# A network on one core: start-up loads in landing order, one weight block at a time in the first feed-forward, latent scores in pairs, copies before reciprocals

## The chip, the core and the metric

One NeuronCore of a Trainium2 chip runs the whole program in one launch. TensorE multiplies, VectorE, ScalarE and GpSimd do the elementwise work, and the queue of SyncE (SP) starts nearly all loads. The metric is device time in microseconds (us): median of 3 runs of the kernel before 2950.37 us (2949.48 to 2950.72).

## The reference

Two large blocks (`first_block`, layers l = 0, 1) and then four smaller mixer layers, on 256 tokens of width 1024, in float32. The parts that the change touches:

```python
# first_block, per layer
mod = silu(c) @ ada_w[l] + ada_b[l]          # (1024) x (1024, 9216): 9 vectors, shift/scale/gain of three norms
h = rms_norm(x) * norm_ffn1[l] * (1 + sc1) + sh1
x = x + 0.5 * (1 + g1) * ((silu(h @ ffn1_w1[l]) * (h @ ffn1_w3[l])) @ ffn1_w2[l])
...
# mla: 8 heads, latent attention; q, k have 128 plain and 64 rotary dimensions per head
s = causal(q @ k.T) * 192 ** -0.5;  p = softmax(s);  o = p @ v
# second part: i = 0..3, mixers NSA, MOBA, short convolution, NSA; in NSA 16 heads x 2 branches
# (selected and window) = 32 score jobs, in MOBA 16 heads = 16 jobs of head dimension 64
```

## The kernel before

**Weights.** Every weight matrix comes in units of 1 MB (a slab of 1024 x 256), in one list `units` in the order of use. `sync_program` walks through the list: unit u goes into `raw[u % 4]` as soon as unit u - 4 is used up (`freed`). A "split" unit is then converted: ScalarE rounds it into the high half of `wsp` (`ready_act`), VectorE subtracts to get the low half (`ready_dve`; in the trace "TENSOR_TENSOR wsp<-raw,wsp"), and TensorE multiplies with high and low halves. There are three `wsp` buffers. `reach(u)` says how far along the list the conversions may go when unit u has been multiplied; it is computed once and gives both engines their order.

**The adaLN units.** `ada_w` makes 72 units (j = 0..71). The first eight are the first units of the list. Even ones (`fresh`) go straight from `raw` to TensorE in `ada_pe` (64 matmul records of one column each, "P<-sm,raw"); odd ones are summed on VectorE in eight steps into an accumulator (`ada_step`, "ACC<-raw,sm"), and TensorE only turns the result (four matmuls, "P<-C,ACC"). `mod_dve` adds the bias; after j = 7 the shift and scale of the first norm are there. So each of the first loads is freed by TensorE (even j, semaphore `AMM`) or VectorE (odd j, `ARED`). Before the change TensorE takes them as 0, 1, 2, ... 7, and VectorE starts on j = 1 only after the reciprocal of the first norm.

**First feed-forward.** `norm_dve` makes the normalised input in chunks (h_scaled, then high part on ScalarE, low part on VectorE; the marks `HLO`). `ffn_pe` multiplies block i of `w1` and `w3` (`f1`, `f3`); for i = 0 it takes both blocks at once through `lins`: chunk by chunk, both weight units per chunk. PSUM banks are handed out in a fixed order by `take`, `take2` and `give`; a bank comes with the marks that must have been reached before it is written.

**Latent attention (MLA).** 8 jobs, one per head. `attend_pe` is software-pipelined by steps i: scores of job i (two products, of 128 contraction rows and of 64 rows, each for 256 and for 128 columns), transposes of the softmax of job i - 3, values of job i - 4. VectorE takes scale, mask and row minimum (L88, "CUSTOM_DVE_ANT_0") and the reciprocal of the sum, ScalarE the exponential and the copy of the transposed tile, GpSimd the scaling (L79). The rotary part of head h lies on partitions 0 to 63 for even h and 64 to 127 for odd h.

**NSA and MOBA attention.** `attend2_pe/act/dve` take two jobs per step; here VectorE also copies the transposed tiles (L94, "arena<-P 128x384"). Its order per job: row minimum, reciprocal of the job before, copy of job i - 4, and at the last job of a chunk the low part of the output of job i - 6 ("GX<-P,GX").

Every engine's program is written out in this order; there is no run-time scheduler.

Of the kernel before, what the change touches and what calls it, by code (L numbers as in the profile page):

```python
# [109 lines left out]
def build(nc, A, cst, out):  # L110
    ctx = ExitStack()
    with ctx:
# [188 lines left out]
        def reach(u):  # L301

            s, a, r = sum(x <= u for x in splits), sum(x <= u for x in U["ada"]), u
            while r + 1 < len(units):
                x = r + 1
                if x in nsplit and nsplit[x] - NS >= s or units[x][3] == "ada" and nada[x] - 2 >= a:
# [70 lines left out]

        def ada_step(e, j, q):
# [3 lines left out]
            if q == 0:  # L382
                e.wait_ge(*RAW[u % NR].at(u))
                e.wait_ge(*COND_.at("cond"))
                if j >= 2:
                    e.wait_ge(*AMM.at(j - 2))
                e.tensor_scalar(ACC[j % 2][:, :], w[:, 0, :], COND[:, 0:1], None, ALU.mult).then_inc(*ARED.up((j, 0)))
            else:
                e.wait_ge(*ARED.at((j, q - 1)))
                e.scalar_tensor_tensor(ACC[j % 2][:, :], w[:, q, :], COND[:, q:q + 1], ACC[j % 2][:, :], ALU.mult,  # L390
# [214 lines left out]
        def start_dve(e):  # L605
# [8 lines left out]
            for q in (1, 2):  # L614
                square_dve(e, 0, q)
            root_dve(e, 0)
            ready_dve(e, -1)
# [67 lines left out]
        def ada_pe(e, j):  # L685
# [11 lines left out]
            else:  # L697
                e.wait_ge(*ARED.at(j))
                e.wait_ge(*c_in.at("c"))
                for q in range(2):  # L700
                    for x in range(2):
                        ins = e.matmul(P[b][half(x), q:q + 1], ACC[j % 2][:, 128 * q + 64 * x:128 * q + 64 * x + 64], one,
# [90 lines left out]
        def spread_pe(e, n):  # L793
# [5 lines left out]
            give(("nspr", n), NR_.at(n) if late(n) else HT_.at((n, 3)))  # L799
# [93 lines left out]
        def ffn_pe(e, f, n):  # L893
            for i in range(NB):
# [880 lines left out]
        def attend_pe(e, a, jobs, base, steps=None):  # L1775

            SM_, PP, PT = att_tiles(base)
            n = len(jobs)
            for i in steps or range(n + 4):
                if i < n:  # L1780
                    j = jobs[i]
                    b = take(e, ("as", a, i))
                    for m in j["after"]:
                        e.wait_ge(*m)
                    last = len(j["q"]) - 1
# [4 lines left out]
                    ins.then_inc(*ASCO.up((a, i)))  # L1790
                    give(("as", a, i), AMX.at((a, i, 1)))
# [150 lines left out]
        def attend2_dve(e, a, jobs, base, scale, steps):  # L1942
            SM_, PP, PT = att_tiles(base)
            n = len(jobs)
            for i in (x for s in steps for x in (2 * s, 2 * s + 1)):
                if i < n:
# [13 lines left out]
                if 4 <= i < n + 4:  # L1960
                    t = i - 4
                    e.wait_ge(*ATR.at((a, t)))
                    if t >= 4:
                        e.wait_ge(*AVL.at((a, t - 4)))
                    e.tensor_copy(PT[t % 4], P[bank["at", a, t]][:, 0:384]).then_inc(*ACPV.up((a, t)))
                if i >= 6 and jobs[i - 6]["last"]:
                    ch = jobs[i - 6]["chunk"]
                    e.wait_ge(*AHI.at((a, ch)))
                    e.tensor_tensor(gL[:, ch, :], P[bank["av", a, ch]][:, 0:256], gH[:, ch, :].bitcast(F32),
                                    ALU.subtract).then_inc(*ALO.up((a, ch)))  # L1970
# [50 lines left out]
        def mla_pe(e, l):  # L2021
# [94 lines left out]
        def mla_act(e, l):  # L2116
# [57 lines left out]
            attend_act(e, l, jobs, 9728, range(0, 2))  # L2174
            ready_act(e, U["gb", l][2])
            gate_b_act(e, l, 3)
            for i in range(2, 12):
# [551 lines left out]
        def tensor_program(e):  # L2729
# [3 lines left out]
            for j in range(8):  # L2733
# [3 lines left out]
                if j == 1:  # L2737
                    spread_pe(e, 0)
# [187 lines left out]
```

## Time and profile before

| | |
|---|---|
| median of 3 runs | 2950.37 us |
| profiled execution, its own time | 2951.04 us |
| its span | 2949.2 us |
| mean granted TensorE clock | 0.981 of full |
| TensorE / weight load / VectorE / ScalarE / GpSimd busy | 96% / 85% / 71% / 49% / 5% |
| chain that ended last | TensorE 83%, VectorE 9%, ScalarE 5%, DMA 1% |

The start of the span is where the first loads and the first norm stand: the first large matmul begins at 52.73 us. The two MLA attentions begin near 567.6 and 1360.4 us, the attentions of the four mixer layers near 1716, 2043 and 2670 us (the short convolution has none). A timeline row gives the start, the length, engine, line of the code (a helper's line, so tiles tell more), operation, out<-in, how many instructions are merged (xN), and in brackets the idle time before it with what ended it. A matmul in float32 leaves two records (two passes).

### The profile page before, as it was taken

To read this page: it belongs to the slowest core of one execution; us is meant where nothing else is said; L and a number is where in the kernel's file an instruction comes from. 1 tells how busy PE (TensorE), PEld (TensorE's weight loads), DVE (VectorE), ACT (ScalarE), POOL (GpSimd) and SP (SyncE) were. 2 spreads that over 40 slices of the span, in tenths; PEclk is the share of its full clock that TensorE was granted. 3 is DMA by queue.
4 is the path that set the end of the run, shared out by engine and by line. 5 is a ranking of instruction groups with operands and counts; after the bars stand their busy time and mean duration, and the time that the engine had idled before them with its cause. 6 is when DMAs were issued, how large, how long until landed. Compare 5 with 4: busy or idle time off the path is not lost.

```text
span 2949.2 us, 53560 instructions
## 1 busy us (share of the span) xinstructions
PE 2826.3 (96%) x22724; PEld 2513.7 (85%) x22724; DVE 2083.9 (71%) x3259; ACT 1457.5 (49%) x1957; POOL 150.7 (5%) x257
## 2 busy tenths in 40 slices
PE   5999999999999999999999999999899999999998
PEld 5888899888888888998888878889788988887887
DVE  5986857668778868666776587754676677657774
ACT  2545644555445466445454365543554345436552
POOL 1000000200000000002000040000100000005000
PEclk9999999999999999999999999999999999999999
DMA  8775337538768753364475624554365556562452
GB/s 260 253 248 171 115 106 217 180 115 258 245 207 261 243 158 116 122 209 158 157 230 184 196 81 143 183 188 144 115 200 185 173 157 199 174 207 67 157 184 102
DMA packets 516702, 521.41 MB, mean 177 GB/s; under 512 B 16503, under 2 KB 513728, under 8 KB 516464
## 3 DMA queue, kind: packets, MB, share of 16 engines
q1 hardware_dynamic: 513856, 517.28, 54.8%
q8 instruction: 180, 2.95, 0.4%
q0 software_dynamic: 816, 0.27, 0.1%
q10 hardware_dynamic: 1792, 0.44, 0.1%
q14 instruction: 58, 0.48, 0.0%
HBM read 516.90 MB, written 1.05 MB: 176 GB/s over the span
## 4 chain that ended last, share of the span: by engine, by line
PE 83%; DVE 9%; ACT 5%; issue 2%; DMA 1%; POOL 0%; ACTq 0%; DVEq 0%; SPq 0%; POOLq 0%
PE P L65 81%; DVE wsp L74 3%; ACT wsp L71 2%; PE P L68 2%; DVE arena L82 1%; ACT arena L71 1%; DVE ACC L82 1%; DVE arena L74 1%; DVE X L74 1%; DMA raw<-in_nsa_w_in 1%; ACT HX L71 1%; ACT L71 0%; DVE HX L82 0%; DVE X L82 0%; DMA raw<-in_ada_w 0%
## 5 line engine op out<-in xcount | busy, mean ns | idle before, releaser
L65 PE MATMUL P<-HX,wsp 128*128 128x256 f32 (+1 forms) x10304 | 1610.2, 318 | 36.2 <-DVE wsp L74 13.9
L65 PEld LDWEIGHTS P<-HX,wsp 128*128 128x128 f32 x10304 | 1451.3, 192 | 174.8 <-issue 22.6
L74 DVE TENSOR_TENSOR wsp<-raw,wsp 128x2048 fp32r<-128x2048 f32 (+4 forms) x440 | 946.1, 2153 | 363.4 <-ACT wsp L71 362.9
L71 ACT ACTIVATE wsp<-raw 128x2048 fp32r<-128x2048 f32 (+4 forms) x440 | 791.1, 1800 | 541.9 <-PE P L65 470.1
L65 PE MATMUL P<-FG,wsp 128*128 128x256 f32 (+1 forms) x2816 | 496.1, 337 | 1.7 <-DVE wsp L74 1.7
L65 PEld LDWEIGHTS P<-FG,wsp 128*128 128x128 f32 x2816 | 428.5, 188 | 64.9 <-DVE wsp L74 2.9
L71 ACT ACTIVATE arena<-P 128x512 f32<-128x512 f32 (+3 forms) x384 | 215.0, 568 | 513.9 <-PE P L65 510.6
L74 DVE TENSOR_TENSOR arena<-arena,P 128x512 f32<-128x512 f32 (+2 forms) x232 | 151.0, 653 | 182.5 <-ACT arena L71 153.5
L65 PE MATMUL P<-arena 64*64 64x64 f32 (+9 forms) x4000 | 235.0, 259 | 9.7 <-DVE arena L74 3.4
L82 DVE SCALAR_TENSOR_TENSOR ACC<-raw,sm,ACC 128x256 f32<-128x256 f32 x476 | 230.8, 485 | 16.7
L65 PEld LDWEIGHTS P<-arena 64*64 64x64 f32 (+3 forms) x4000 | 185.7, 145 | 55.6 <-issue 29.8
L65 PE MATMUL P<-GX,wsp 128*128 128x256 f32 (+1 forms) x1592 | 229.7, 304 | 2.9 <-DVE GX L74 2.9
L65 PEld LDWEIGHTS P<-GX,wsp 128*128 128x128 f32 x1592 | 211.8, 192 | 16.1 <-DVE GX L74 3.5
L79 POOL TENSOR_SCALAR arena<-arena,sm 128x128 f32<-128x128 f32 x192 | 101.9, 542 | 1310.4 <-DVE sm L97 1307.7
L71 ACT ACTIVATE arena<-arena 128x512 f32<-128x512 f32 (+2 forms) x177 | 107.3, 614 | 15.6 <-DVE arena L74 11.8
L71 ACT ACTIVATE arena<-arena,sm 128x128 f32<-128x128 f32 x192 | 85.5, 447 | 59.0 <-DVE sm L88 56.6
L74 DVE TENSOR_TENSOR arena<-arena 128x512 f32<-128x512 f32 x147 | 100.7, 689 | 16.4 <-ACT arena L71 12.9
L71 ACT ACTIVATE FG<-arena 128x512 fp32r<-128x512 f32 x88 | 55.7, 633 | 104.3 <-DVE arena L74 103.9
L68 PE MATMUL P<-C,arena 128*128 128x128 f32 x410 | 69.1, 299 | 28.9 <-POOL arena L79 12.2
L65 PEld LDWEIGHTS P<-C,arena 128*64 128x64 f32 (+1 forms) x1712 | 58.0, 142 | 33.0 <-ACT arena L71 21.5
L65 PE MATMUL P<-C,arena 128*64 128x1 f32 (+1 forms) x1712 | 64.0, 204 | 22.2 <-ACT arena L71 20.3
L71 ACT ACT_TABLE_LOAD x60 | 77.0, 1283 | 16.8 <-issue 10.2
(110 smaller groups left out, 1375.0 us busy)
## 6 DMA issues: line engine op xcount, KB each, us to landing
raw<-in_ffn_w SPq DMA_DIRECT2D x120, 1024.0 KB, 5.3
raw<-in_ada_w SPq DMA_DIRECT2D x72, 1024.0 KB, 5.1
raw<-in_w_in SPq DMA_DIRECT2D x52, 1024.0 KB, 5.2
raw<-in_ffn_w_gate SPq DMA_DIRECT2D x44, 1024.0 KB, 5.3
raw<-in_ffn_w_up SPq DMA_DIRECT2D x44, 1024.0 KB, 5.3
raw<-in_ffn_w_down SPq DMA_DIRECT2D x32, 1024.0 KB, 5.1
raw<-in_nsa_w_in SPq DMA_DIRECT2D x20, 1024.0 KB, 7.0
raw<-in_ffn_w SPq DMA_DIRECT2D x16, 768.0 KB, 4.4
```

The lines of the kernel that those rows point to most:

```text
L65: return self if self.e is None else self.e.matmul(*a, skip_group_check=True, **k)
L68: return self if self.e is None else self.e.transpose(*a)
L71: return self if self.e is None else self.e.activation(*a, **k)
L74: return self if self.e is None else self.e.tensor_tensor(*a)
L79: return self.e.tensor_scalar(o, a, s1, None, op0) if op1 is None else self.e.tensor_scalar(o, a, s1, s2, op0, op1)
L82: return self if self.e is None else self.e.scalar_tensor_tensor(out=o, in0=a, scalar=s, in1=b, op0=op0, op1=op1)
```

## The change

Four parts. (1) The eight first adaLN units are taken by TensorE in the order 0, 2, 1, 4, 3, 6, 5, 7; VectorE sums j = 1 and j = 3 before the reciprocal of the first norm; the odd units alternate between the two accumulators. (2) In the first block of the first feed-forward of layer 0 (f = 0 only), TensorE multiplies the `f1` unit alone, chunk by chunk, and then the whole `f3` unit; the bank of the norm's spread goes to the end of the line of free banks. (3) In MLA the scores of jobs i and i + 1 are multiplied together at even i, product by product; the first four jobs (before: two) come before the third gate product. (4) In NSA and MOBA VectorE's copy of job i - 4 stands ahead of the reciprocal of job i - 1, and the low part of the output comes one job later.

```diff
@@ reach: how far the conversions may run ahead
-                if ... or units[x][3] == "ada" and nada[x] - 2 >= a:
+                if ... or units[x][3] == "ada" and nada[x] - (4 if nada[x] < 8 else 2) >= a:
@@ ada_step (and ada_pe: ACC[j % 2] becomes acc(j))
+        def acc(j):
+            return ACC[j // 2 % 2 if j < 8 else j % 2]
-                if j >= 2:
-                    e.wait_ge(*AMM.at(j - 2))
-                e.tensor_scalar(ACC[j % 2][:, :], w[:, 0, :], COND[:, 0:1], None, ALU.mult).then_inc(*ARED.up((j, 0)))
+                if j >= 4:
+                    e.wait_ge(*AMM.at(j - 4 if j < 8 else max(7, j - 2)))
+                e.tensor_scalar(acc(j)[:, :], w[:, 0, :], COND[:, 0:1], None, ALU.mult).then_inc(*ARED.up((j, 0)))
@@ start_dve
+            ready_dve(e, -1)
             root_dve(e, 0)
-            ready_dve(e, -1)
@@ spread_pe: for n = 0 the bank is given back later, in tensor_program
-            give(("nspr", n), NR_.at(n) if late(n) else HT_.at((n, 3)))
+            if n:
+                give(("nspr", n), NR_.at(n) if late(n) else HT_.at((n, 3)))
@@ ffn_pe, i == 0
-                    lins(e, us, ps, HX, h_pairs(n), (lambda: sums_pe(e, n)) if late(n) else None)
+                    if f == 0:
+                        lins(e, us[0:1], ps[0:1], HX, h_pairs(n))
+                        lin_wide(e, us[1], ps[1], HX).then_inc(*MM.up(us[1]))
+                    else:
+                        lins(e, us, ps, HX, h_pairs(n), (lambda: sums_pe(e, n)) if late(n) else None)
@@ tensor_program
-            for j in range(8):
+            for j in (0, 2, 1, 4, 3, 6, 5, 7):
                 ada_pe(e, j)
                 if j == 0:
                     sums_pe(e, 0)
-                if j == 1:
+                if j == 3:
                     spread_pe(e, 0)
+            give(("nspr", 0), HT_.at((0, 3)))
@@ attend_pe: the scores
-                if i < n:
-                    ...
-                    for x, (q, k) in enumerate(j["q"]):
-                        e.matmul(P[b][:, 128:384], q[:, 128:256], k, start=x == 0, stop=x == last)
-                    for x, (q, k) in enumerate(j["q"]):
-                        ins = e.matmul(P[b][:, 0:128], q[:, 0:128], k[:, 0:128], start=x == 0, stop=x == last)
+                if i < n and i % 2 == 0:
+                    ...
+                    for x in range(2):
+                        for t in (i, i + 1):
+                            q, k = jobs[t]["q"][x]
+                            e.matmul(P[bank["as", a, t]][:, 128:384], q[:, 128:256], k, start=x == 0, stop=x == 1)
+                    for x in range(2):
+                        for t in (i, i + 1):
+                            q, k = jobs[t]["q"][x]
+                            ins = e.matmul(P[bank["as", a, t]][:, 0:128], q[:, 0:128], k[:, 0:128], start=x == 0, stop=x == 1)
@@ attend2_dve: the block below moves in front of the reciprocal
+                if 4 <= i < n + 4:
+                    t = i - 4
+                    e.wait_ge(*ATR.at((a, t)))
+                    if t >= 4:
+                        e.wait_ge(*AVL.at((a, t - 4)))
+                    e.tensor_copy(PT[t % 4], P[bank["at", a, t]][:, 0:384]).then_inc(*ACPV.up((a, t)))
                 if 1 <= i <= n:
                     ...
                     e.reciprocal(RC[:, c:c + 2], SUM[:, c:c + 2]).then_inc(*ARC.up((a, i - 1)))
-                (the same copy)
-                if i >= 6 and jobs[i - 6]["last"]:
+                for t in (i - 7, i - 6) if i == n + 5 else (i - 7,):
+                    if 0 <= t < n and jobs[t]["last"]:
@@ mla_pe (mla_act: range(0, 3); mla_dve: range(0, 4))
-            attend_pe(e, l, jobs, 9728, range(0, 2))
+            attend_pe(e, l, jobs, 9728, range(0, 3))
             gate_pe(e, l, "b", 3)
             spread_head_pe(e, l, 7)
-            attend_pe(e, l, jobs, 9728, range(2, 12))
+            attend_pe(e, l, jobs, 9728, range(3, 12))
```


On TensorE at the very start, before (raw: even j straight from the load; ACC: odd j; `C,arena 64x1`: sums of the first norm; `C,sm 128x128`: its spread):

```order
L68 MATMUL P<-C,arena 128x128 x19
L65 MATMUL P<-sm,raw 64x1 x32
L65 MATMUL P<-C,arena 64x1 x16
L65 MATMUL P<-C,ACC 64x1 x4
L68 MATMUL P<-C,sm 128x128 x2
L65 MATMUL P<-sm,raw 64x1 x32
L65 MATMUL P<-C,ACC 64x1 x4
L65 MATMUL P<-sm,raw 64x1 x32
```

The same place now:

```order
L68 MATMUL P<-C,arena 128x128 x19
L65 MATMUL P<-sm,raw 64x1 x32
L65 MATMUL P<-C,arena 64x1 x16
L65 MATMUL P<-sm,raw 64x1 x32
L65 MATMUL P<-C,ACC 64x1 x4
L65 MATMUL P<-sm,raw 64x1 x32
L65 MATMUL P<-C,ACC 64x1 x4
L68 MATMUL P<-C,sm 128x128 x2
```

The product of j = 2 no longer stands behind the sum of j = 1, and the spread of the norm comes after j = 3.

On VectorE at the start, as a difference (COPY X: the input; `arena<-arena`: squares of the first norm; ACC: the adaLN sums):

```order
 L74 TENSOR_TENSOR arena<-arena 128x512 x2
-L97 RECIPROCAL sm<-sm 128x2
-L79 TENSOR_SCALAR ACC<-raw,sm 128x256
-L82 SCALAR_TENSOR_TENSOR ACC<-raw,sm,ACC 128x256 x7
+L79 TENSOR_SCALAR ACC<-raw,sm 128x256
+L82 SCALAR_TENSOR_TENSOR ACC<-raw,sm,ACC 128x256 x7
+L79 TENSOR_SCALAR ACC<-raw,sm 128x256
+L82 SCALAR_TENSOR_TENSOR ACC<-raw,sm,ACC 128x256 x7
+L97 RECIPROCAL sm<-sm 128x2
```

Two sums now stand ahead of the reciprocal, which TensorE's spread waits for.

On TensorE in the latent attention of layer 0, as a difference (`C,sm`: spread of a head norm; `arena 128x256`, `128x128`: scores and values; `C,arena 128x128 x3`: transposes; `HX,wsp x48`: the third gate product):

```order
 L65 MATMUL P<-C,arena 64x1 x16
-L65 MATMUL P<-arena 128x256 x2
-L65 MATMUL P<-arena 128x128 x2
-L65 MATMUL P<-arena 128x256 x2
-L65 MATMUL P<-arena 128x128 x2
+L65 MATMUL P<-arena 128x256 x4
+L65 MATMUL P<-arena 128x128 x4
+L65 MATMUL P<-arena 128x256 x4
+L65 MATMUL P<-arena 128x128 x4
 L65 MATMUL P<-HX,wsp 128x256 x48
 L68 MATMUL P<-C,sm 128x128 x4
```

Four score jobs, in two pairs, now stand ahead of the gate product, where two stood.

## Rows read from the trace of the kernel before

**Rows 1.** Page, part 1: busy time of each engine
```profile
PE 2826.3 (96%) x22724; PEld 2513.7 (85%) x22724; DVE 2083.9 (71%) x3259; ACT 1457.5 (49%) x1957; POOL 150.7 (5%) x257
```

**Rows 2.** Timeline of TensorE, 0 to 75: start, length, line, operation, count [idle before]
```profile
52.73 1.65 PE L65 MATMUL P<-HX,wsp 128*128 128x512 f32 x4 [7.37 <-DVE arena L82]
56.80 12.74 PE L65 MATMUL P<-HX,wsp 128*128 128x512 f32 x60 [2.41 <-DVE wsp L74]
```

**Rows 3.** Timeline of TensorE, 69 to 185
```profile
69.80 11.42 PE L65 MATMUL P<-HX,wsp 128*128 128x512 f32 x64
...
106.19 11.38 PE L65 MATMUL P<-HX,wsp 128*128 128x512 f32 x64 [1.33 <-ACT PC L71]
...
118.47 11.39 PE L65 MATMUL P<-HX,wsp 128*128 128x512 f32 x64 [0.57 <-DVE wsp L74]
```

**Rows 4.** Timeline of the load queue (SP), 25 to 27 and 30 to 32
```profile
25.88 0.37 SPq L103 DMA_DIRECT2D raw<-in_ada_w  x1
...
30.76 1.00 SPq L103 DMA_DIRECT2D raw<-in_ada_w  x2
```

**Rows 5.** DMA view, 0 to 80: GB/s in 40 slices of 2 us
```profile
GB/s 11 227 387 159 339 321 332 323 347 346 250 373 26 115 380 39 297 373 347 345 350 348 349 349 352 387 369 155 16 305 232 274 371 343 39 0 0 146 379 146
```

**Rows 6.** Timeline of VectorE, 0 to 75
```profile
17.59 1.50 DVE L74 TENSOR_TENSOR arena<-arena 128x512 f32<-128x512 f32 x2 [2.52 <-ACT arena L71]
...
45.68 2.28 DVE L74 TENSOR_TENSOR wsp<-raw,wsp 128x2048 fp32r<-128x2048 f32 x1
47.88 1.65 DVE L82 SCALAR_TENSOR_TENSOR arena<-X,AB,P 128x256 f32<-128x256 f32 x4
...
60.57 2.28 DVE L74 TENSOR_TENSOR wsp<-raw,wsp 128x2048 fp32r<-128x2048 f32 x1
...
71.31 2.29 DVE L74 TENSOR_TENSOR wsp<-raw,wsp 128x2048 fp32r<-128x2048 f32 x1 [1.11 <-ACT wsp L71]
```

**Rows 7.** Timeline of ScalarE, 0 to 75
```profile
43.63 1.91 ACT L71 ACTIVATE wsp<-raw 128x2048 fp32r<-128x2048 f32 x1 [21.90 <-DMA raw<-in_ffn_w]
```

**Rows 8.** Windows: stretch, length, TensorE busy (instructions), clock, DMA share, GB/s
```profile
1382.67:1383.20 0.53, 0.53 (x4) 1.00 0.00 0
1383.20:1383.83 0.63, 0.63 (x4) 1.00 0.00 0
1383.83:1384.24 0.41, 0.41 (x3) 1.00 0.00 0
1384.24:1384.66 0.42, 0.42 (x3) 1.00 0.00 0
2055.35:2056.20 0.85, 0.85 (x9) 1.00 0.00 0
```

**Rows 9.** Windows, the latent attention of layer 1, all engines
```profile
1360.38:1393.42 33.04, 31.28 (x176) 23.06 (x173) 19.66 (x64) 18.60 (x52) 6.62 (x16) 1.00 0.35 114
```

**Rows 10.** Timeline of VectorE, 565 to 610
```profile
578.38 3.61 DVE L82 SCALAR_TENSOR_TENSOR ACC<-raw,sm,ACC 128x256 f32<-128x256 f32 x7
...
595.16 0.29 DVE L88 CUSTOM_DVE_ANT_0 arena<-P,C 128x128 f32<-128x128 f32 x1 [1.45 <-PE P L65]
```

**Rows 11.** Timeline of ScalarE, 565 to 610
```profile
596.39 0.47 ACT L71 ACTIVATE arena<-P 128x384 f32<-128x384 f32 x1
```

**Rows 12.** Waits of TensorE in MOBA, 2069 to 2087: total, times, longest
```profile
PE P L68 <- POOL arena L79: 2.8, 1, 2.8
PE P L68 <- DVE sm L88: 2.5, 1, 2.5
```

**Rows 13.** Waits of TensorE in the first NSA attention, 1733 to 1757
```profile
PE P L68 <- POOL arena L79: 4.2, 5, 0.8
```

**Rows 14.** Timeline of VectorE, 1733 to 1757.5
```profile
1740.16 0.42 DVE L74 TENSOR_TENSOR GX<-P,GX 128x256 fp32r<-128x256 f32 x1 [0.45 <-ACT GX L71]
...
1742.84 0.17 DVE L97 RECIPROCAL sm<-sm 128x2 f32<-128x2 f32 x1 [0.62 <-ACT arena L71]
```

**Rows 15.** Timeline of GpSimd, 1733 to 1757.5
```profile
1743.10 3.02 POOL L79 TENSOR_SCALAR arena<-arena,sm 128x128 f32<-128x128 f32 x2 [0.80 <-DVE sm L97]
```

More of the change, by code:

```diff
@@ L305, in reach @@
                 x = r + 1
-                if x in nsplit and nsplit[x] - NS >= s or units[x][3] == "ada" and nada[x] - 2 >= a:
+                if x in nsplit and nsplit[x] - NS >= s or units[x][3] == "ada" and nada[x] - (4 if nada[x] < 8 else 2) >= a:
                     break
@@ L701, in ada_pe @@
                     for x in range(2):
-                        ins = e.matmul(P[b][half(x), q:q + 1], ACC[j % 2][:, 128 * q + 64 * x:128 * q + 64 * x + 64], one,
+                        ins = e.matmul(P[b][half(x), q:q + 1], acc(j)[:, 128 * q + 64 * x:128 * q + 64 * x + 64], one,
                                        start=True, stop=True)
@@ L1779, in attend_pe @@
             for i in steps or range(n + 4):
-                if i < n:
[L1781 to L1785, printed above, removed]
-                    for x, (q, k) in enumerate(j["q"]):
-                        e.matmul(P[b][:, 128:384], q[:, 128:256], k, start=x == 0, stop=x == last)
-                    for x, (q, k) in enumerate(j["q"]):
-                        ins = e.matmul(P[b][:, 0:128], q[:, 0:128], k[:, 0:128], start=x == 0, stop=x == last)
-                    ins.then_inc(*ASCO.up((a, i)))
-                    give(("as", a, i), AMX.at((a, i, 1)))
+                if i < n and i % 2 == 0:
+                    for t in (i, i + 1):
+                        take(e, ("as", a, t))
+                        for m in jobs[t]["after"]:
+                            e.wait_ge(*m)
+                    for x in range(2):
[3 more added lines that the diff above has]
+                    for x in range(2):
+                        for t in (i, i + 1):
+                            q, k = jobs[t]["q"][x]
+                            ins = e.matmul(P[bank["as", a, t]][:, 0:128], q[:, 0:128], k[:, 0:128], start=x == 0, stop=x == 1)
+                            if x:
+                                ins.then_inc(*ASCO.up((a, t)))
+                    for t in (i, i + 1):
+                        give(("as", a, t), AMX.at((a, t, 1)))
                 if 3 <= i < n + 3:
@@ L1959, in attend2_dve @@
                     e.reciprocal(RC[:, c:c + 2], SUM[:, c:c + 2]).then_inc(*ARC.up((a, i - 1)))
[L1960 to L1965, printed above, removed]
-                if i >= 6 and jobs[i - 6]["last"]:
[L1967 to L1970, printed above, removed]
+                for t in (i - 7, i - 6) if i == n + 5 else (i - 7,):
+                    if 0 <= t < n and jobs[t]["last"]:
+                        ch = jobs[t]["chunk"]
+                        e.wait_ge(*AHI.at((a, ch)))
+                        e.tensor_tensor(gL[:, ch, :], P[bank["av", a, ch]][:, 0:256], gH[:, ch, :].bitcast(F32),
+                                        ALU.subtract).then_inc(*ALO.up((a, ch)))
         def att_pairs(a):
@@ L2173, in mla_act @@
             e.wait_ge(*MPL.at((l, "rope", 3)))
-            attend_act(e, l, jobs, 9728, range(0, 2))
+            attend_act(e, l, jobs, 9728, range(0, 3))
             ready_act(e, U["gb", l][2])
             gate_b_act(e, l, 3)
-            for i in range(2, 12):
+            for i in range(3, 12):
                 attend_act(e, l, jobs, 9728, [i])
@@ L2226, in mla_dve @@
             jobs, scale = mla_jobs(l), 192.0 ** -0.5
-            attend_dve(e, l, jobs, 9728, scale, range(0, 2))
+            attend_dve(e, l, jobs, 9728, scale, range(0, 4))
             ready_dve(e, U["gb", l][2])
             norm_head_dve(e, l, 7)
-            for i in range(2, 12):
+            for i in range(4, 12):
                 attend_dve(e, l, jobs, 9728, scale, [i])
```

2 lines of the change are left out of this document (1 added, 1 removed).

## Prediction

> **What bounds the kernel now.** First the page's busy times [rows 1]: TensorE is busy 96% of the span, so a change pays only where TensorE stands still or its own work gets shorter. Then the timelines, for the places where it stands. At the start the first large matmuls begin at 52.73; 4 of them run, then TensorE waits until 56.80 for a weight conversion [rows 2]. From 69.80 it is dense, but for waits of 1.33 and 0.57 us at 106.19 and 118.47 [rows 3]. In MLA it has 31.28 busy of 33.04 us [rows 9], so only shorter work helps there. In MOBA and NSA it waits for VectorE and GpSimd: 2.8 + 2.5 us and 4.2 us in the middle of each attention [rows 12, 13].
>
> **Part 1, landing order.** Load u + 4 starts when u is freed. Load 5 starts at 25.88, when the sum of j = 1 is done, and 6 and 7 at 30.76 [rows 4]. In the gap the stream falls to 26, 115 and 39 GB/s, and again to 297 (slices 13 to 17) [rows 5]: in 24 to 32 us 1.12 MB came where some 350 GB/s would bring 2.8, so about 4.8 us are lost. Now the sum of j = 1 starts behind the squares, at 17.59 + 1.50 = 19.1 [rows 6]; the eight steps take 4.0 us (one of 0.35, seven in 3.61 as at 578.38 [rows 10]), so it is done at 23.1: load 5 starts 2.8 us earlier. The product of j = 2 follows the norm's sums and frees load 6 at about 25.0; the sum of j = 3 frees load 7 at 27.1. Load 5's data come some 1.4 us after its issue (25.88 to the 115 GB/s slice), at 24.5, so 0.3 to 0.5 us of gap stay: gain 4.4, after which every issue is early enough that the stream runs through. The first weight unit, which landed at 43.63 [rows 7], lands at 39.2. Conversion high 1.9, low 2.2: the norm's chunks start at 43.4 instead of 47.88 [rows 6]. The last adaLN sum (j = 7, landed near 35.5, 4.0 us) is done at 39.5 and its bias at 40.3, just in front of the low conversion; 1 us more of landing would cost 0.5. I take 4.5 (3 to 5.5). The reciprocal moves from 21.8 to 27.1; its only reader is needed when the chunks start, 16 us later: no cost. The other queues (ScalarE's, GpSimd's) have issued all they hold by then.
>
> **Part 2, first block alone.** All times now from T0, the start of the chunks (47.88 before). TensorE's first matmul came at +4.85, because the bank of the spread was the first in line and is free only after the last chunk; then it waited for the second unit's low half until +8.9, and was done at +21.9 (69.80). The 60 records took 12.74, at the dense rate of rows 3 (11.35 / 64 = 0.177) they would take 10.6: about 12 ran at the 1.2 GHz level. Now f1 can start at +2.1 (chunk 0's low part). 32 records: the clock rose some 4 us into the dense stretch, 8 us after the first matmul; I take 5 us: 14 at 0.354, 18 at 0.177, end at +10.3. The last chunk is ready at +6.7, so no chunk is waited for. f3's low half is ready at +8.9 as before, 32 records, end at +16.0. TensorE goes on with the second block at 16.3 instead of 21.9: gain 5.6 (4 to 6.5). Is the next unit there? Its low conversion started at 60.57 and ended at +15.0 [rows 6]: 1.3 us to spare.
>
> What is late next: VectorE's own chain. Before, it restarted at 71.31 with the conversion that waited for f1's end (+23.4), and ran without a break up to the rotary table; the waits at 106.19 and 118.47 hang on its end [rows 3]. f1 now ends at +10.3, so that conversion follows the one of +15.0 after one PSUM addition, at +15.7: with part 1 the chain is 12.2 us earlier, TensorE only 10.1. The 1.9 us of waits therefore go too. Per block VectorE needs 10.9 us (two conversions 4.4, eight adaLN steps 4.0, four small operations 2.5) and TensorE 11.7 (11.35 and the adaLN matmuls), so VectorE holds its lead. Parts 1 and 2: 4.5 + 5.6 + 1.9 = 12.0. Bounds 7 (the two waits stay, low ends) to 14.
>
> **Part 3, score pairs.** One job's scores are four groups, 0.53 + 0.63 + 0.41 + 0.42 = 1.99 us [rows 8]. The two passes of 256 columns in 64 rows cost 0.21 more than those of 128: two more passes of 256 cost 0.42, of 128 0.21, without a new changeover. In a pair the 64-row products of the two heads lie in different halves; MOBA's 64-row pairs take 0.85 for both jobs, less than one job's 0.63 + 0.42 [rows 8], so they run side by side. Pair: 0.53 + 0.42 + 0.63 + 0.41 + 0.21 + 0.42 = 2.62 against 3.98. Four pairs: 5.4 us of TensorE work less per layer. That is the upper bound, and more only if present waits (1.8 us, rows 9) go as well.
>
> Not all of it arrives. The softmax of one job runs VectorE, ScalarE, VectorE, GpSimd. The minimum starts at 595.16 and ScalarE is free for its copy at 596.39 [rows 10, 11]: 1.2 us, then copy 0.4, output's high part 0.4, VectorE's low part 0.4, next minimum 0.55: a round of about 2.75 per job, 5.5 per pair, since the low part stands in front of the next minimum. TensorE's step pair is 2.62 + 2 x 1.04 (transposes and values: step 3.03 - 1.99) = 4.7, before 6.1. So the loop of the other engines becomes the bound: 0.6 per pair instead of 1.35, about 2 us over the later pairs. In front, four jobs ahead of the gate product give 2.7 whole. But VectorE has a conversion and an adaLN sum (578.38, 3.61) and a head norm to do [rows 10] before the minimum of job 4, and ScalarE's copy of job 1 stands behind job 4's exponential: TensorE waits some 2 us there, in place of the present 0.65 and 0.41. Written out step by step, layer 1's 33.04 become 28.9: 4.1 per layer, 8.2 for both. Bounds: 1 (each saving waits for the loop) to 6 per layer.
>
> **Part 4, copies first.** In NSA's middle the reciprocal waits 0.62 for an exponential [rows 14], behind a weight conversion on ScalarE; the copy (0.46) stood behind it and now fills that wait. The loop VectorE - ScalarE had a period of 8.14 and loses 0.46 a round, three rounds; but where the reciprocal does not wait, it now comes 0.5 later, and GpSimd and TensorE's transposes with it: 1.4 - 0.5 = 0.9 per NSA. In MOBA the low part waited 0.45 in every pair, as in NSA [rows 14] (now a job later, no wait), and two reciprocals 0.62: written out, the last reciprocal comes 2.0 earlier; TensorE's 5.3 us of waits [rows 12] shrink by 2.0. Sum 3.8; bounds -2 (all 64 + 16 reciprocals late by 0.46 where GpSimd is waited for, some 4 places) to 6.
>
> GpSimd's two scalings took 3.02 us beside VectorE's weight subtraction [rows 15], against 1.0 elsewhere; the subtraction now starts 0.1 us behind the reciprocal, in front of the scaling. The Trainium skill (GPSIMD Engine Reference, its specification table) says the same: the SBUF interfaces are shared with VectorE, and an operation with two SBUF inputs contends. Without that contention the sum of part 4 would be about 5; the trace agrees with the rule, so 3.8 stands.
>
> **Sum.** 12.0 + 8.2 + 3.8 = 24.0. The profiled execution took 2951.04, which gives 2927.0; the median of the runs lies 0.7 below it, 2926.4. I say 2927.
>
> **Rivals.** (a) The pairs are eaten by the softmax loop, and the copies bring nothing: parts 1 and 2 give 12, part 3 2, part 4 0: 2936. For it: the engines hand over four times per job, and ScalarE has fixed places. Against: in front of the gate 2.7 us are pure work. (b) The start gives back: VectorE's chain, not TensorE, sets the second block, or landing stays late: parts 1 and 2 give 6 instead of 12: 2933. For it: only 1.3 us to spare at +15.0. (c) The change does not do what it says: the 64-row products do not run side by side, since here they accumulate onto a full-row product. The pair then takes 2.62 + 0.42 + 0.21 = 3.25, the changeovers saved remain: 0.7 per pair, 2.9 less per layer; part 3 gives 4: 2931. (d) Slower: TensorE's clock. In MLA TensorE's share falls from 31.3 of 33.0 to some 26 of 29, in bursts; should the grant fall to the 1.2 GHz level for the whole of both attentions, each gets some 26 us longer: 2927 + 52 = 2979. It decides from 48 us at the low level more than before. For it: the mean clock of 0.981 means that some 112 us of the span (0.019 x 2949 x 2) run at the low level already. Against: in the MLA of layer 1, with gaps of the same kind, it stayed at 1.00 [rows 9].
>
> The Trainium skill (TensorE: Matmul & The Clock Gate, HAM oscillation) describes bursts of matmuls with waits between that keep throttling the array; it would speak for (d), and rows 9 do not agree so far.
>
> **How the numbers follow.** Forecast 70% (own range 2920 to 2932), (a) 8%, (b) 9%, (c) 8%, (d) 3%, others 2%. The low end: 14 + 11 + 5 = 30 gives 2920, and one low-clock stretch less (6.8 us at half, 3.4) 2918. The high end: (a) with one stretch more, 2940. A measurement tells 0.2%, 6 us, from no change; only (d), and the low bounds of all parts together (7 + 2 - 2 = 7, just beyond), come near: faster 0.94, same 0.03, slower 0.03.
>
> **What would show it.** The first large matmul near 45.5; the second block's first near 59.7; no wait at the fourth and fifth blocks; conversion of the first unit near 39.2; in MLA the stretch from first score to first branch product near 29 us in layer 1, with the 64-row records of two jobs starting within 0.01 us; MOBA's last transpose wait under 1 us. Wrong if the first block's end moves by less than 8 us, or MLA by less than 3 per layer, or if the clock column of MLA falls below 0.9 in both layers.

## The result: 2934.8 us, 0.5% faster, two thirds of the forecast gain

The changed kernel takes 2934.79 us (median; 2933.52 to 2937.44) against 2950.55 for the kernel before on the same chip: ratio 0.9949, 95% interval 0.9936 to 0.9962, so 11 to 19 us. A second series gave 0.9940 [0.9927, 0.9952]. Forecast: 2927, that is 24 us. The result is 8 us short of it: outside the forecast's own range of 2920 to 2932, and inside the whole one of 2918 to 2940. The start brought slightly more than forecast (12.9 us against 12.0); the score pairs brought 1.7 us by the stages below instead of 8.2. The ratios are of fast executions alone; one execution of `copies_only` below took 5588.85 us and is in none of them.

Page of the kernel after, part 1, which answers to [rows 1]:

```profile
PE 2811.5 (96%) x22724; PEld 2507.6 (86%) x22724; DVE 2082.6 (71%) x3259; ACT 1457.1 (50%) x1957; POOL 154.4 (5%) x257
```

TensorE has 14.8 us less busy time. TensorE's timeline at the start, after, answers to [rows 2, 3]:

```profile
44.63 12.92 PE L65 MATMUL P<-HX,wsp 128*128 128x512 f32 x64 [4.82 <-DVE HX L82]
...
57.81 11.42 PE L65 MATMUL P<-HX,wsp 128*128 128x512 f32 x64
...
93.30 11.39 PE L65 MATMUL P<-HX,wsp 128*128 128x512 f32 x64 [0.43 <-ACT PC L71]
...
105.58 11.38 PE L65 MATMUL P<-HX,wsp 128*128 128x512 f32 x64 [0.55 <-DVE wsp L74]
```

The first block runs through without the wait of 2.41, the second starts 12.0 us earlier than at 69.80, and the block that stood at 118.47 12.9 earlier. Three things set it, and the next rows show them: VectorE's two early sums and the chunks of the norm (from 42.33, before 47.88), ScalarE's first conversion, and the load stream. The rows are from timelines and the DMA view of 0 to 80, and answer to [rows 5 to 7]. VectorE's conversion at 57.82 is the one that stood at 71.31.

```profile
18.86 3.61 DVE L82 SCALAR_TENSOR_TENSOR ACC<-raw,sm,ACC 128x256 f32<-128x256 f32 x7
...
22.97 3.61 DVE L82 SCALAR_TENSOR_TENSOR ACC<-raw,sm,ACC 128x256 f32<-128x256 f32 x7
26.50 0.16 DVE L97 RECIPROCAL sm<-sm 128x2 f32<-128x2 f32 x1
...
42.33 1.65 DVE L82 SCALAR_TENSOR_TENSOR arena<-X,AB,P 128x256 f32<-128x256 f32 x4
...
57.82 2.28 DVE L74 TENSOR_TENSOR wsp<-raw,wsp 128x2048 fp32r<-128x2048 f32 x1
```

```profile
38.03 1.91 ACT L71 ACTIVATE wsp<-raw 128x2048 fp32r<-128x2048 f32 x1 [17.06 <-DMA raw<-in_ffn_w]
```

```profile
GB/s 14 223 387 151 341 319 331 329 345 346 349 304 350 344 347 350 330 359 339 352 346 351 382 371 294 50 225 299 211 376 345 347 347 351 237 382 253 305 243 311
```

The stream has no hole between 24 and 48 us any more. Now the latent attention (MLA), both layers from first score to first branch product; windows with the columns of [rows 9] (PE, PEld, DVE, ACT, POOL, clock, DMA share, GB/s):

```profile
554.44:588.26 33.82, 29.01 (x177) 23.16 (x174) 20.23 (x66) 18.64 (x52) 6.64 (x16) 0.90 0.33 111
1349.62:1383.40 33.78, 28.97 (x177) 23.12 (x174) 20.23 (x66) 18.61 (x52) 6.64 (x16) 0.90 0.34 111
```

33.8 us each, where [rows 9] had 33.04 for layer 1 and 28.9 was forecast. TensorE is busy for 2.3 us less, but it waits for 4.8 instead of 1.8, and the mean clock is 0.90. In layer 0 the kernel before took 36.2 in its first profile, with a low stretch of the clock, and 33.0 in its second. TensorE's timeline of layer 1, after:

```profile
1368.30 5.04 PE L65 MATMUL P<-arena 128*128 128x256 f32 x20 [2.30 <-ACT arena L71]
...
1375.22 0.89 PE L65 MATMUL P<-arena 128*128 128x256 f32 x4 [0.42 <-ACT arena L71]
...
1378.54 1.01 PE L65 MATMUL P<-arena 128*128 128x256 f32 x4 [2.10 <-ACT arena L71]
```

All three are waits for ScalarE's copy of a transposed tile. Its timeline shows what stood in front of it:

```profile
1366.80 0.40 ACT L71 ACTIVATE arena<-arena,sm 128x128 f32<-128x128 f32 x1 [3.69 <-DVE sm L88]
...
1367.69 0.47 ACT L71 ACTIVATE arena<-P 128x384 f32<-128x384 f32 x1
...
1375.23 1.91 ACT L71 ACTIVATE wsp<-raw 128x2048 fp32r<-128x2048 f32 x1
1377.04 0.40 ACT L71 ACTIVATE arena<-arena,sm 128x128 f32<-128x128 f32 x1
...
1377.91 0.48 ACT L71 ACTIVATE arena<-P 128x384 f32<-128x384 f32 x1
```

The first long wait is for the copy of job 1 (1367.69). It stands behind job 4's exponential, ahead of which ScalarE idled 3.69 us for VectorE's minimum. The second is for the copy of job 4 (1377.91), behind a weight conversion of 1.91 and job 7's exponential. The kernel before has the same conversion in front of the same copy, but TensorE waited only 0.71 for it (ScalarE and TensorE, before, layer 1):

```profile
1386.63 1.90 ACT L71 ACTIVATE wsp<-raw 128x2048 fp32r<-128x2048 f32 x1
...
1389.93 0.89 PE L65 MATMUL P<-arena 128*128 128x256 f32 x4 [0.71 <-ACT arena L71]
```

TensorE alone, after, in stretches around the waits (windows; last the clock, DMA share, GB/s):

```profile
1368.30:1368.90 0.60, 0.60 (x3) 1.00 1.07 382
1368.90:1372.30 3.40, 3.40 (x12) 0.50 0.16 55
1379.10:1382.50 3.40, 3.40 (x15) 0.51 0.00 0
566.57:569.23 2.66, 2.66 (x19) 1.00 0.78 238
```

0.6 us after each of the two long waits the granted clock falls to the 1.2 GHz level, for 3.4 us of dense work: 1.7 us lost each time. The last row is one pair of scores at full clock: 2.66 us for two jobs, forecast 2.62, before 3.98 (2 x 1.99, [rows 8]).

The table shows where the time went by stage, in us, from the profiles of this study. A stage runs from its first large matmul to the next stage's. In brackets stands half of the time at the 1.2 GHz level inside it, which is what that level costs dense work; where TensorE waits anyway it costs less. MLA counts here from the gate product ahead of the first score, some 7.4 us earlier than that score:

| stage | before | before, second profile | start only | after | both moves | low part later |
|---|---|---|---|---|---|---|
| start to MLA 0 | 560.2 | 559.5 | 546.5 | 547.0 | 546.7 | 547.3 |
| MLA 0 | 43.6 (3.4) | 40.4 (0) | 42.1 (3.4) | 41.2 (3.4) | 37.6 (0) | 33.9 (0) |
| on to MLA 1 | 749.1 (10.2) | 749.6 (10.2) | 753.2 (13.7) | 753.9 (15.4) | 753.7 (15.4) | 749.2 (10.2) |
| MLA 1 | 40.5 (0) | 40.4 (0) | 42.1 (3.4) | 41.2 (3.4) | 37.6 (0) | 33.9 (0) |
| first NSA | 136.2 (6.8) | 135.0 (3.4) | 136.1 (6.8) | 133.9 (5.1) | 133.9 (5.1) | 135.3 (6.8) |
| MOBA | 106.4 (7.4) | 105.6 (8.1) | 105.4 (5.1) | 104.4 (6.2) | 104.4 (6.1) | 104.5 (6.1) |
| second NSA | 135.6 (6.8) | 134.7 (5.1) | 134.5 (5.1) | 135.1 (6.8) | 133.6 (5.1) | 133.6 (5.1) |

After against before: start 13.2, MLA 0 2.4, on to MLA 1 -4.8, MLA 1 -0.7, first NSA 2.3, MOBA 2.0, second NSA 0.5, the other stages 2.6 together: 17.5, of which the clock's stretches moved several us in both directions.

### The profile page after: what moved, and what is told of

Its sections match the earlier page's. It is cut to its first block and busy times, and to the rows that moved or that the text cites. A ratio compares the mean times of both kernels' runs of the same rounds, so it can differ in the third digit from the quotient of the medians.

```text
span 2931.7 us, 53561 instructions
## 1 busy us (share of the span) xinstructions
PE 2811.5 (96%) x22724; PEld 2507.6 (86%) x22724; DVE 2082.6 (71%) x3259; ACT 1457.1 (50%) x1957; POOL 154.4 (5%) x257
## 3 DMA queue, kind: packets, MB, share of 16 engines
q8 instruction: 180, 2.95, 0.4%
## 5 line engine op out<-in xcount | busy, mean ns | idle before, releaser
L65 PE MATMUL P<-arena 64*64 64x64 f32 (+9 forms) x4000 | 226.3, 260 | 14.1 <-ACT arena L71 9.6
L79 POOL TENSOR_SCALAR arena<-arena,sm 128x128 f32<-128x128 f32 x192 | 105.6, 561 | 1296.1 <-DVE sm L97 1293.7
L65 PEld LDWEIGHTS P<-C,arena 128*64 128x64 f32 (+1 forms) x1712 | 57.8, 141 | 33.9 <-ACT arena L71 21.5
L65 PE MATMUL P<-C,arena 128*64 128x1 f32 (+1 forms) x1712 | 63.9, 204 | 23.1 <-ACT arena L71 20.3
```

Source lines behind the costliest of these rows:

```text
L65: return self if self.e is None else self.e.matmul(*a, skip_group_check=True, **k)
L79: return self.e.tensor_scalar(o, a, s1, None, op0) if op1 is None else self.e.tensor_scalar(o, a, s1, s2, op0, op1)
```

## The experiments

Twelve runs, each with a profile: ten other kernels, and the kernels before and after once more. Ratios are to the kernel before on the same chip (its medians are 2948.2 to 2950.6); the groups of runs lie on different chips, so between groups the ratios compare better than the times.

**Parts one at a time.** `landing_only` is the kernel before with part 1 (the order of loads and adaLN sums, the accumulators, VectorE's sums ahead of the reciprocal); `start_only` has parts 1 and 2; `no_pairs` and `no_copies` are the changed kernel without part 3 or part 4; `copies_only` is the kernel before with part 4:

```diff
# landing_only: the hunks of reach, acc, ada_step, VectorE's first ready_dve, and
-            for j in range(8):
+            for j in (0, 2, 1, 4, 3, 6, 5, 7):
# start_only: also the bank of the norm's spread, and in ffn_pe
+                    if f == 0:
+                        lins(e, us[0:1], ps[0:1], HX, h_pairs(n))
+                        lin_wide(e, us[1], ps[1], HX).then_inc(*MM.up(us[1]))
# no_pairs, no_copies, copies_only: the hunks of attend_pe and the MLA ranges, or of attend2_dve
```

> The kernel before with part 1 alone (load order, adaLN sums in landing order). If the landing of the first weight unit sets the start (my step), its conversion starts 5.5 us earlier, near 38.0, the norm's chunks near 42.4, and the first large matmul near 47.2; VectorE's chain and TensorE move by the same 5.5: ratio 0.9981, some 2945. Rival: the freed time turns into a wait for the second unit or for VectorE's chain, and the fifth and sixth blocks start no earlier: within 1 us of before.

Measured: 2945.98, 0.9986 [0.9978, 0.9994], 2 to 6 us. TensorE's timeline and ScalarE's first conversion:

```profile
65.42 11.43 PE L65 MATMUL P<-HX,wsp 128*128 128x512 f32 x64
...
101.80 11.38 PE L65 MATMUL P<-HX,wsp 128*128 128x512 f32 x64 [1.31 <-ACT PC L71]
```

```profile
39.49 1.91 ACT L71 ACTIVATE wsp<-raw 128x2048 fp32r<-128x2048 f32 x1 [18.07 <-DMA raw<-in_ffn_w]
```

4.4 us earlier at both blocks (69.80 and 106.19 before) and 4.1 at the conversion; the two waits stay as they were, since VectorE's chain and TensorE move together. I had expected 5.5 here. The landing varies by 1 to 1.5 us between profiles: the conversion starts at 37.7 to 38.2 in the ten others with this order, and at 42.4 to 43.6 in the three with the old one.

> Parts 1 and 2 alone. Theory: the start gives 13 us and nothing of it is lost later: 2937.5 (0.9956), and the block that started at 118.47 starts near 105.6. Then the score pairs and the copies together are worth only some 3 us of the median. Rival: the start's gain is partly given back later (clock, loads), the pairs being worth their forecast 8: 2943.

Measured: 2937.22, 0.9958 [0.9945, 0.9970]: the theory's number. The gain at the matmul that stood at 448.5 us is 13.6, that of the landing alone 4.8.

> The changed kernel without the score pairs (part 3). Theory: the pairs' pure saving (5 us of TensorE per layer) is eaten by waits behind ScalarE's fixed places and by low-clock stretches, so that they are worth 0 to 3 us over both layers: 2935 to 2938. Rival: they are worth 8 as forecast and something else takes it back: 2943. In the trace the two MLA stretches should be 36 and 33 us, as before.

Measured: 2937.49, 0.9958 [0.9945, 0.9970]. So the pairs are worth 2.7 us on these medians. Against the second series of the changed kernel (0.9940) it would be 5, and the intervals overlap, so the medians leave anything from 0 to 8 open. The stages decide: 41.2 against 42.1 in each layer, 1.9 for both. But the two MLA stretches did not take 36 and 33 us: both took 34.7. This is layer 1, TensorE alone:

```profile
1350.10:1352.20 2.10, 2.10 (x11) 0.98 0.89 290
1352.20:1359.00 6.80, 6.80 (x23) 0.50 0.44 153
1359.00:1384.82 25.82, 25.11 (x145) 1.00 0.25 82
```

6.8 us at the 1.2 GHz level from the third microsecond on, in both layers, without a wait ahead of it. `landing_only` and `start_only`, whose MLA code is that of the kernel before, have the same: the earlier start alone moved this stretch there. A clean attention of the old order takes 33.0 (second profile of before, below), one with this stretch 34.7, the pairs with their waits 33.8.

> The changed kernel without part 4 (VectorE's order in NSA and MOBA as before). Theory: part 4 is worth 4 to 6 us: 2939 to 2941; MOBA's and NSA's waits of TensorE are as in the kernel before. Rival: it is worth nothing by itself (what the later sections gained was the clock): 2935.

Measured: 2934.75, 0.9944 [0.9929, 0.9959], no different from the changed kernel. So the theory was wrong and the rival's number came. This says less than it seems: TensorE waits in the MOBA stage for 10.6 us in all (after: 8.0), and NSA's round is the old one, but this execution had 3.4 us at the low level in the first NSA where that of the changed kernel had 10.2. The part alone tells more:

> The kernel before with part 4 alone. Theory: it shortens TensorE's waits by 0.9 us in each NSA and 0.9 in MOBA, 2 to 3 us in all, and the clock's stretches cover that: 2947 to 2949, not to be told from before. Rival (my forecast): 3.8 us, 2946, with MOBA's last wait gone.

Measured: 2946.92, 0.9985 [0.9976, 0.9994], 2 to 7 us, in which both theories lie. Its waits in MOBA are those of after to the digit. TensorE's waits there, in the kernel after, answer to [rows 12] (total, times, longest):

```profile
PE P L68 <- POOL arena L79: 3.4, 2, 2.9
PE P L68 <- DVE GX L74: 2.2, 1, 2.2
```

The last wait for GpSimd is 2.9 us long as before; my step that MOBA's last wait falls under 1 us is wrong. All waits in the stage of MOBA come to 8.0, in before 9.0 and 8.4 (two profiles), in `start_only` 10.3. In NSA the round did shorten. GpSimd after, answering to [rows 15]:

```profile
1722.57 2.95 POOL L79 TENSOR_SCALAR arena<-arena,sm 128x128 f32<-128x128 f32 x2 [0.92 <-DVE sm L97]
...
1730.22 2.97 POOL L79 TENSOR_SCALAR arena<-arena,sm 128x128 f32<-128x128 f32 x2 [1.21 <-DVE sm L97]
```

7.65 us a round, forecast 8.14 - 0.46 = 7.68. At equal time at the low level (13.6 us in both) the first NSA takes 135.2 in `no_pairs` and 136.1 in `start_only`: 0.9, the forecast number. MOBA takes 104.5 against 105.4, with 2.0 us more at the low level. With half of the low-level time taken off, the new order takes 98.4 there (`no_pairs` and `copies_only` alike), and the old one 97.5, 99.0 and 100.3 (before twice, `start_only`): in MOBA its worth is not settled. Counted with 0.9 for it, and 0.6 in the second NSA (`copies_only` against before, same time at the low level), part 4 is worth 2.4 by its stages, 3.8 forecast.

**Is it the products side by side?** Same slots, but each job's four groups by themselves:

```diff
-                    for x in range(2):
-                        for t in (i, i + 1):
+                    for t in (i, i + 1):
+                        for x in range(2):
# and the same for the products of 128 columns
```

> The changed kernel, but the two jobs of a pair issue their scores one after the other, four groups each, in the same slot. If the side-by-side products are what part 3 earns, TensorE's pair becomes 4.0 us instead of 2.66 and the MLA stretch (first score to first branch product) grows by what of 4 x 1.3 the waits do not hide. Theory (waits behind ScalarE rule): the waits of 2.3, 0.4 and 2.1 us shrink by most of it and the stretch grows by only 1 to 2 us per layer: 2937. Rival (TensorE's work rules): 5 us per layer more: 2945.

Measured: 2949.32, 0.9997 [0.9983, 1.0010], by the ratios 14 to 17 us slower than the changed kernel, beyond both. The executions scatter, though: two of eleven took 2936.5 and 2937.9, as the theory has it, nine 2944.5 to 2952.9. The profile is of one of the nine (2951.76). Windows of layer 1 (all engines, then TensorE alone):

```profile
1357.40:1398.51 41.11, 38.81 (x177) 28.10 (x176) 20.44 (x67) 19.32 (x52) 8.58 (x16) 0.79 0.27 92
```

```profile
1357.40:1359.50 2.10, 2.10 (x14) 1.00 0.81 284
1359.50:1373.20 13.70, 13.70 (x37) 0.51 0.23 77
1373.20:1398.51 25.31, 23.01 (x130) 0.93 0.25 84
```

TensorE is busy 9.8 us more (some 5.3 of it work, 4 x 1.32; most of the rest is 17.1 us at the low level instead of 6.8), its waits fall from 4.8 to 2.3: 7.3 us a layer. The theory was right that waits hide half of the work; both left out the clock. The 13.7 us stretch lies in dense work, at the place where the old order had 6.8.

**The two waits.** Each has a move that takes away what ScalarE does ahead of the copy:

```diff
# copy_first (attend_act): the copy of job 1 ahead of the exponential of job 4
+                if i in (4,):
+                    copy()
# later_conv (mla_act; mla_dve from i == 8 to i == 9)
-                if i == 6:
+                if i == 8:
                     ready_act(e, U["gb", l][3])
# both_moved: both
```

> The changed kernel with ScalarE's copy of job 1 ahead of job 4's exponential. Theory: TensorE's wait of 2.3 us in the middle of each MLA attention goes to under 0.5, the wait of 2.1 at job 4's copy stays; each attention 1.5 to 2 us shorter: 2931. Rival: the wait is VectorE's (conversion, adaLN sum, head norm ahead of job 4's minimum) and only moves two steps on, to job 4's transposes: nothing gained, 2935.

Measured: 2928.85, 0.9939 [0.9927, 0.9952]. The wait of 2.30 becomes 0.46; one of 1.11 appears two steps later, and the 2.10 stays. MLA 1 takes 38.6 instead of 41.2 from the gate product on, with one low stretch less: the theory was right on the wait, and the rival's second wait came at half its size.

> The changed kernel with ScalarE's weight conversion in the attention two jobs later (behind job 5's copy), VectorE's one job later. Theory: TensorE's wait of 2.1 us for job 4's copy goes, 1.5 to 2 us per attention: 2931. Rival: the conversion is then late for the second branch block or the loads behind it, and a wait of 1 us or more stands there instead: 2934.

Measured: 2926.84, 0.9935 [0.9923, 0.9948]. The wait of 2.10 becomes 1.11, and 1.44 stand at job 6's copy; the second branch block is not late, as the theory has it, but only half of the wait is gone. Its two layers are the cleanest pair for the clock: same waits, 2.3 us the longest; in layer 0 the low level followed, in layer 1 not:

```profile
552.46:585.24 32.78, 27.54 (x173) 21.70 (x174) 18.81 (x65) 18.43 (x52) 6.59 (x16) 0.95 0.33 113
1342.09:1373.27 31.18, 25.95 (x173) 20.88 (x174) 18.81 (x65) 18.43 (x52) 6.59 (x16) 1.00 0.36 119
```

> The changed kernel with both of these moves. Theory: both waits go, each attention takes 29 to 30.5 us instead of 33.8, less low-clock time with it: 2927 to 2929. Rival: the softmax loop of VectorE, ScalarE and GpSimd (5.5 us a pair) is the bound behind them; only half comes, 2931 to 2932, and the stretch stays above 31.5.

Measured: 2925.20, 0.9927 [0.9915, 0.9939]. Both layers take 30.15; layer 1:

```profile
1345.34:1375.49 30.15, 26.04 (x176) 20.94 (x174) 18.68 (x66) 18.49 (x52) 6.59 (x16) 1.00 0.39 125
```

This is the theory's number for the stretch (29 to 30.5). The clock is full throughout. Each layer takes 3.6 us less than after, with only 0.7 less waiting (4.1 against 4.8): the rest is the clock. The remaining 4.1 us of waits are the round of the softmax and the conversion, now in front of job 6's copy. The round, on ScalarE and VectorE of this kernel:

```profile
1366.77 0.40 ACT L71 ACTIVATE arena<-arena,sm 128x128 f32<-128x128 f32 x1 [0.70 <-DVE sm L88]
...
1367.66 0.47 ACT L71 ACTIVATE arena<-P 128x384 f32<-128x384 f32 x1
1368.03 0.37 ACT L71 ACTIVATE GX<-P 128x256 fp32r<-128x256 f32 x1
```

```profile
1366.45 0.28 DVE L88 CUSTOM_DVE_ANT_0 arena<-P,C 128x128 f32<-128x128 f32 x1
...
1368.43 0.42 DVE L74 TENSOR_TENSOR GX<-P,GX 128x256 fp32r<-128x256 f32 x1 [1.27 <-ACT GX L71]
1368.78 0.28 DVE L88 CUSTOM_DVE_ANT_0 arena<-P,C 128x128 f32<-128x128 f32 x1
```

From minimum to minimum 2.33 us; VectorE stands 1.27 of them for the high part of the output, which it subtracts ahead of the next minimum. So:

```diff
-                if i >= 4 and jobs[i - 4]["last"]:
-                    ch = jobs[i - 4]["chunk"]
+                for t in (i - 5, i - 4) if i == n + 3 else (i - 5,):
+                    if 0 <= t < n and jobs[t]["last"]: ...
# and ScalarE's conversion from i == 8 to i == 10, VectorE's to i == 11
```

> The kernel with both moves, and in the latent attention also the output's low part one job later on VectorE (behind the next minimum) and ScalarE's weight conversion behind the last job's copy. Theory: the waits of 1.11, 1.11 and 1.44 us that are left are the round minimum, exponential, copy, high part, low part, minimum (2.33 us a job) and the conversion in front of job 6's copy; both go, each attention 2 to 3 us shorter (35 us from gate product to first branch product, against 37.56): 2920 to 2921. Rival: the round is closed elsewhere (ScalarE's own order, GpSimd's scaling), or the conversion is late for the second branch block: within 1 us of the kernel with both moves, 2925.

Measured: 2919.01, 0.9901 [0.9883, 0.9919], the fastest kernel of the study, 29 us ahead of before and 12 to 15 ahead of the change. Both layers of MLA from first score to first branch product, and TensorE's waits there:

```profile
554.71:581.16 26.45, 25.74 (x177) 20.96 (x174) 18.27 (x66) 16.88 (x52) 6.56 (x16) 1.00 0.42 142
1337.82:1364.27 26.45, 25.74 (x176) 20.96 (x174) 18.27 (x66) 16.87 (x52) 6.57 (x16) 1.00 0.42 143
```

```profile
PE P L65 <- ACT arena L71: 0.7, 2, 0.4
```

TensorE is busy 25.74 at full clock, against 31.28 in [rows 9]: the pairs take away 5.5 us of work per layer (5.4 forecast), and here 6.6 arrive.

**The same program twice.**

> The kernel before, unchanged, for a second profile. Theory (the clock's low stretches fall differently in executions of one program): up to the large matmuls of 448 us all instructions stand within 0.5 us of the first profile, but stages later differ by 1.5 to 3.5 us each where a low stretch falls or not. Rival (the places of the low stretches belong to the program): all stages within 0.5 us.

Measured: 2943.84 (one run). Up to MLA 0 it stands within 0.7 us of the first profile. Later only MLA 0 differs much, by 3.2 us: the 6.8 us stretch at the low level is missing there:

```profile
566.87:599.89 33.02, 31.29 (x176) 23.05 (x174) 19.62 (x65) 18.58 (x52) 6.56 (x16) 1.00 0.34 113
```

Five of the later stages differ by 0.8 to 1.4 each, the others by 0.6 at most: less than the theory had. Up to 1500 us six of the seven low stretches stand at the same instructions in both profiles; after that several differ in place or length. So a part of them differs between executions of one and the same program.

> The changed kernel, unchanged, in the same rounds as the others: 2932 to 2936. Theory: its profile shows again waits of 2.3, 0.4 and 2.1 us in each MLA attention, with low-clock stretches at or near them but not at the same places; the stretch from gate product to first branch product is 37.8 us plus half of the low-clock time in it. Rival: the low stretches belong to the waits, and stand at the same places in both layers.

Measured: 2931.99, 0.9940 [0.9927, 0.9952]. Waits of 2.3, 0.4 and 2.1 in both layers; the low stretches stand again 0.4 to 0.6 us behind the two long waits: the rival was right. Over all profiles here, 18 waits of 2.1 to 2.3 us fell into MLA attentions (four each in `after`, `after_again` and `no_copies`, two each in `one_by_one`, `copy_first` and `later_conv`), and at 17 of them a low stretch of 3.4 us began between 0.6 us before the wait's end and 1.2 us after it. At the waits of 1.1 and 1.4 us (12, in `copy_first`, `later_conv` and `both_moved`) none began.

This holds for the MLA attentions and not for the rest of the kernel. In the same fourteen profiles 80 other waits of 2.05 to 2.45 us began at full clock. At 59 of them a low stretch began during the wait or within 1.2 us after it, at 21 none, among them the wait of 2.2 us in MOBA in each of the nine profiles that have it. Of 235 other waits of 0.9 to 1.5 us, 46 were followed by one. Why the attentions are more regular is not shown.

The Trainium skill (TensorE: Matmul & The Clock Gate, "A second HAM failure mode") tells of a kernel in which short idle gaps between groups of matmuls made the clock swing between its two levels. The traces of the MLA attentions agree, and give the price there: a wait of 2.1 us, with 1.7 lost in the 3.4 us at the low level behind it, cost 3.8.

## Why the prediction was right at the start and wrong in the middle

- **Landing order: 4.5 forecast; right.** 4.4 measured alone, 5.5 in the profile of after with 1 us of varying landings. VectorE's sums were done at 22.5 and 26.6 (forecast 23.1 and 27.1), the conversion stood at 39.5 and 38.0 (39.2). The start of the chunks adds up to 43.3 (39.2 + 1.9 + 2.2), not to the 43.4 that was written.
- **First block alone: 5.6 forecast; right.** From the start of the chunks, the first matmul came at +2.3 (forecast +2.1) and the second block at +15.5 (+16.3): a gain of 6.4. The clock rose 3.3 us into the block, where I took 5.
- **The two waits gone, 1.9: half right.** They fell from 1.33 and 0.57 to 0.43 and 0.55, 0.9 us. Parts 1 and 2 together: 12.9 measured, 12.0 forecast.
- **Pair of scores: right.** 2.66 us (2.62), 5.5 us of work less per layer (5.4); the 64-row products of the two jobs do run side by side, their records 0.01 us apart. Rival (c) falls.
- **MLA 33.04 becomes 28.9: the step that failed.** 25.9 us of work (31.28 - 5.4) and 3.0 of waits were forecast; it was 25.7 of work, 4.8 of waits and 3.2 of clock. The first wait, "some 2 us" for ScalarE's copy of job 1, is there with 2.30. The prediction nowhere counts ScalarE's conversion at step 6: 1.91 us on an engine whose copy TensorE waits for, which became 2.10 of wait. Before, with 6.1 us a pair, there was room for all but 0.71 of it. And each long wait took 1.7 more by the clock, for which the sum had nothing. Two of the prediction's own signs of being wrong bear on it. MLA was to move by at least 3 per layer: layer 1 got 0.7 longer, and layer 0 only 2.4 shorter. And the clock column was not to fall below 0.9 in both layers: it stands at 0.90 in both. `copy_first`, `later_conv` and `both_moved` show the two waits and the clock by taking them away.
- **The loop of 5.5 per pair: too slow.** It took 2.33 per job, 4.7 per pair. It did bound, but only once the other two were gone, and only through VectorE's low part in front of the minimum; that I had put in the loop rightly, and `low_later` removed it.
- **Copies first: 3.8 forecast; 0.9 in NSA right, 2.0 in MOBA not shown.** The last wait in MOBA stayed at 2.9. The part is worth 2.4 by the stages, 4.4 [1.8, 7.1] by the runs of the part alone. GpSimd's contention stayed (2.97), as forecast.
- **Rivals.** (a) named 2936 and 2 us for the pairs, nearly what came, but for another reason: not the round, but fixed jobs of ScalarE. (d), the clock, came in small: 3.2 us a layer. The argument against it was layer 1 at clock 1.00 "with gaps of the same kind"; those gaps were 0.4 to 0.7 us, the new ones 2.1 to 2.3. That was the error: not the same kind.
- **Not forecast at all:** between the two attentions the changed kernel loses 4.8 us, with 10.2 us more at the low level (10.2 to 15.4, in halves), and so does every kernel with the new start (4 to 5 us) except `later_conv` and `low_later`. The code there is unchanged. One of the added stretches, 6.8 us from 1065.1 on, begins at the end of a wait that the kernel before has too, without a stretch (TensorE, after and before):

```profile
1065.31 1.02 PE L65 MATMUL P<-C,arena 128*64 128x1 f32 x16 [2.36 <-ACT arena L71]
...
1078.89 0.63 PE L65 MATMUL P<-C,arena 128*64 128x1 f32 x16 [2.36 <-ACT arena L71]
```

Nine of the fourteen profiles have a stretch at this wait, and they are the nine that lose 4 to 5 us here; the other five have none. Why it falls in some kernels only stays open; that the stretches move when earlier code ends at another time is all that these runs show.

Against the forecast 6.5 us are missing in part 3 (8.2 against 1.7 by the stages), 4.8 here and 1.4 in part 4, 12.7 in all. That the total is only 8 short is in part luck: the start gave 1 us more than its term, and the rest came back in stages where nothing was forecast or where low stretches fell otherwise.

## What to carry to other kernels

When work on the bounding engine gets shorter, write out every job of the engines that hand to it over that stretch, weight conversions and whatever else stands at a fixed step among them; a job that was hidden can become a wait of its full length (here 0.71 us of wait became 2.10, for a job of 1.91). A wait of 2 us in the middle of these attentions cost nearly 4, so a saving that opens such waits can lose: against the clean old order (33.0) the pairs with their waits (33.8) did. Moving one copy and one conversion then gave 7 us by the stages, more than the pairs had brought. And compare stages that have the same time at the low level: that told 0.9 us apart in NSA where the medians could not. Taking half of the low-level time off is a cruder tool; in MOBA it gave 97.5 to 100.3 us for one and the same order.

## What the runs showed of the hardware

- In the MLA attentions a wait of 2.1 to 2.3 us of TensorE came with 3.4 us at the 1.2 GHz level in 17 of 18 cases; one of 1.1 to 1.4 us in none of 12. Elsewhere it was 59 of 80 (2.05 to 2.45 us) and 46 of 235 (0.9 to 1.5 us).
- The low level also falls in dense stretches with no wait over 0.25 us in the 9 us ahead: 6.8 us in `no_pairs`, 13.7 in `one_by_one`, at the same place of both layers. With `landing_only`, which changes only the start, such a stretch of 6.8 us stands 2 us behind the first score in both layers; in the two profiles of before it does not.
- Products of 64 rows on different halves of the array run side by side in float32 although each adds to a full-row product: 64-row records of the two jobs start 0.01 us apart.
- GpSimd's pair of scalings takes 2.95 to 3.02 us beside VectorE's weight subtraction, before and after; without it 0.99 in NSA and 0.83 in MLA.
